# Expert 0's first 64 rows chosen on chip by matmul, and the token rows' scaling moved from VectorE to ScalarE, in an encoder layer with a mixture of experts

## The reference, cut to what matters

```
x = x + concat(attention outputs) @ w_out
h = rmsnorm(x) * ffn_norm
gl = h @ router_group + bias          # 4 groups, the best one
el = h @ router_expert + bias         # 32 experts, the best two of the 8 in that group
out = sum over the two of gate * (silu(h @ w_gate[e]) * (h @ w_up[e])) @ w_down[e]
y = rmsnorm(x + out) * final_norm
```

## Time and profile before

| | us |
|---|---|
| Runs (3): median, lowest, highest | 811.28, 810.48, 814.19 |
| The profiled execution: its own time | 814.31 |
| its span | 812.6 |
| TensorE busy in it | 721.4 |

### The profile page before, as it was taken

The page is one execution under the profiler, slowest core; times in us unless marked ns, Lnnn a source line. Parts: engine busy times, 40 slices in busy tenths (PEclk is TensorE's granted clock), DMA queues, the critical chain, the costliest instruction groups (busy, mean ns, idle before and its releaser), DMA issues. The chain is left out here.

```text
span 812.6 us, 12300 instructions
## 1 busy us (share of the span) xinstructions
PE 721.4 (89%) x3978; PEld 406.1 (50%) x3979; DVE 321.7 (40%) x900; ACT 214.0 (26%) x575; POOL 201.1 (25%) x478
## 2 busy tenths in 40 slices
PE   6799999999978999999999964999998999999910
PEld 3455544444455666665555543555554555555500
DVE  3853221100088988881555561111121112112138
ACT  2432210111176777771211110111110111111122
POOL 1133332220024230232001223441231434442110
PEclk9999999999999999999999976999998999999965
DMA  8702002000050000000892168899999989999856
GB/s 301 293 1 104 0 1 89 15 0 1 9 204 1 1 1 1 2 2 0 327 419 83 79 225 296 292 343 372 394 341 383 378 293 360 405 370 396 352 219 258
DMA packets 40824, 154.64 MB, mean 190 GB/s; under 512 B 9642, under 2 KB 10794, under 8 KB 31936
## 3 DMA queue, kind: packets, MB, share of 16 engines
q1 hardware_dynamic: 33120, 138.20, 45.3%
q0 software_dynamic: 7648, 15.75, 5.7%
HBM read 142.29 MB, written 20.03 MB: 200 GB/s over the span
## 5 line engine op out<-in xcount | busy, mean ns | idle before, releaser
L1405 PE MATMUL banks<-arena 128*128 128x512 f32 (+1 forms) x384 | 164.5, 582 | 10.2 <-DMA arena<-w_in 7.7
L1670 PE MATMUL banks<-arena 128*64 128x256 f32 x1280 | 155.2, 388 | 5.7 <-issue 2.4
L1670 PEld LDWEIGHTS banks<-arena 128*64 128x64 f32 x1280 | 96.1, 139 | 52.5 <-issue 13.8
L1405 PEld LDWEIGHTS banks<-arena 128*128 128x128 f32 x384 | 72.5, 194 | 86.4 <-issue 79.0
L1679 PE MATMUL banks<-arena 128*64 128x512 f32 x320 | 94.4, 609 | 0.5 <-ACT arena L980 0.5
L1561 PE MATMUL banks<-arena 128*128 128x512 f32 x192 | 86.4, 598 | 1.1 <-DVE arena L1162 1.1
L1326 DVE TENSOR_TENSOR arena<-arena,banks 128x128 f32<-128x128 f32 x40 | 11.5, 288 | 165.4 <-ACT arena L972 165.4
L1118 DVE TENSOR_REDUCE arena<-banks 128x1 f32<-128x512 f32 (+1 forms) x96 | 55.3, 598 | 48.5 <-PE banks L1477 41.5
L903 ACT ACTIVATE arena<-banks,arena 128x512 f32<-128x512 f32 (+1 forms) x96 | 58.2, 611 | 42.6 <-DVE arena L1121 20.6
L1561 PEld LDWEIGHTS banks<-arena 128*128 128x128 f32 x192 | 35.1, 190 | 38.8 <-issue 37.5
L972 ACT ACTIVATE arena<-banks 128x128 f32<-128x128 f32 x40 | 11.1, 277 | 159.0 <-PE banks L1670 159.0
(11 more groups left out here) (179 smaller groups left out, 855.6 us busy)
## 6 DMA issues: line engine op xcount, KB each, us to landing
arena<-w_gate SPq DMA_DIRECT2D x32, 1024.0 KB, 12.7
arena<-w_up SPq DMA_DIRECT2D x32, 1024.0 KB, 12.8
arena<-w_down SPq DMA_DIRECT2D x32, 1024.0 KB, 13.0
arena<-w_in SPq DMA_DIRECT2D x3, 2048.0 KB, 8.3
arena<-pair_rows SPq DMA_DIRECT2D x5, 1024.0 KB, 11.2
arena<-w_out SPq DMA_DIRECT2D x1, 4096.0 KB, 12.8
arena<-xT SPq DMA_DIRECT2D x6, 512.0 KB, 10.2
arena<-x SPq DMA_DIRECT2D x6, 512.0 KB, 10.5
```

The lines of the kernel that those rows point to most:

```text
L1405: last = nc.tensor.matmul(bank(mm % 2)[:, 0:GROUP_COLS[g]], xgT[:, t, c, :], w[:, c, :], start=(c == 0), stop=(c == DC - 1))
L1670: last = nc.tensor.matmul(bank(b)[h * SLOTS:(h + 1) * SLOTS, 0:2 * P].rearrange("p (g n) -> p g n", g=2), x_eT[i][:, c, :], w[:, :, c, h * ...
```

## The change

The store of scaled rows loses its gain and moves to ScalarE; the gain is multiplied in when rows are copied out behind their transposes. Expert 0's first 64 rows no longer come by a gather. For each tile, VectorE makes `select` (128 tokens x 64 slots): the one-hot slot, times the token's mask of expert 0, times its rs. TensorE multiplies x_tok by it, summed over six tiles in bank 4, the left 512 columns in partitions 0 to 63 and the right in 64 to 127. ScalarE copies that to x_sel; 16 matmuls with the identity transpose it; VectorE multiplies by the gain. On SP, expert 31's load is now issued ahead of the wait for the scattered lists and of their load. TensorE reads the counts behind the transposes of expert 1. The rest is the same; some tiles change places in SBUF (left out).

```diff
@@ SP
+                    sp.dma_start(gain_rows, A["ffn_norm"].rearrange("o (p c) -> (o p) c", c=DC)).then_inc(lam_loaded, 16)
...
-            sp.dma_start(gain_ffn, A["ffn_norm"].to_broadcast([P, D])).then_inc(gffn_in, 16)
...
             store_residual(NT - 1)
+            sp.wait_ge(x2_stored, NT * 16)
+            sp.wait_ge(h2_ready, NT)
+            sp.wait_ge(rms2_ready, NT)
+            sp.wait_ge(x2T_psum, 2 * NT)
+            sp.wait_ge(chosen_psum, 1)
+            load_expert(NGRP - 1, members(NGRP - 1)[-1])
             sp.wait_ge(ids_scattered, 2 * NT * 16)
             for h in range(2):
                 sp.dma_start(yids_sb[h * SLOTS:(h + 1) * SLOTS, NE:].rearrange("r (b e) -> r b e", e=NE),
                              ids_dram.rearrange("(b r e) o -> r b (e o)", b=NBLK, e=NE)[:, 1:, :]).then_inc(ids_loaded, 16)
-            sp.wait_ge(x2_stored, NT * 16)
-            sp.wait_ge(h2_ready, NT)
-            sp.wait_ge(rms2_ready, NT)
-            sp.wait_ge(x2T_psum, 2 * NT)
-            load_expert(NGRP - 1, members(NGRP - 1)[-1])
@@ GpSimd
-            gather_main(0, 0)
+            pool.sem_inc(id_ready, 1)
             gather_main(0, 1)
@@ ScalarE
+            def ffn_norm(t):
+
+                act.wait_ge(norm_ready, t + 1)
+                if t >= 2:
+                    act.wait_ge(h2_stored[t % 2], 16 * (t // 2))
+                act.activation(h2[t % 2].rearrange("n (c p) -> n c p", c=DC), x_tok[:, t, :].rearrange("n (p c) -> n c p", c=DC),
+                               ACT.Copy, scale=rs[:, t:t + 1]).then_inc(h2_ready, 1)
+
...
                 if t < NT - 1:
                     x2T_evac(t)
+                ffn_norm(t)
+            act.wait_ge(chosen_psum, 1)
+            act.activation(x_sel, bank(4), ACT.Copy).then_inc(chosen_rows, 1)
             act.wait_ge(gates_in, 1)
@@ VectorE
-                dve.wait_ge(lam_loaded, 6 * 16)
+                dve.wait_ge(lam_loaded, 7 * 16)
...
-            def ffn_norm(t):
+            def norm(t):
                 dve.wait_ge(rms2_ready, t + 1)
-                link(dve.reciprocal(rs[:, t:t + 1], rs[:, t:t + 1]))
...
-                dve.scalar_tensor_tensor(h2[t % 2].rearrange("n (c p) -> n c p", c=DC),
-                                         x_tok[:, t, :].rearrange("n (p c) -> n c p", c=DC), rs[:, t:t + 1],
-                                         gain_ffn.rearrange("n (p c) -> n c p", c=DC), ALU.mult, ALU.mult).then_inc(h2_ready, 1)
+                dve.reciprocal(rs[:, t:t + 1], rs[:, t:t + 1]).then_inc(norm_ready, 1)
+                dve.wait_ge(norm_ready, t + 1)
...
+            def choose(t):
+
+                for i, mask in enumerate((m1_all, m2_all)):
+                    dve.tensor_scalar(share[:, i:i + 1], mask[:, t, 0:1], rs[:, t:t + 1], None, ALU.mult).then_inc(dve_chain, 1)
+                    chain[0] += 1
+                dve.wait_ge(dve_chain, chain[0])
+                dve.wait_ge(onehot_ready, 2 * t + 2)
+                link(dve.tensor_scalar(select[:, t, :], onehot[:, 0, 0:SLOTS], share[:, 0:1], None, ALU.mult))
+                dve.scalar_tensor_tensor(select[:, t, :], onehot[:, 1, 0:SLOTS], share[:, 1:2], select[:, t, :],
+                                         ALU.mult, ALU.add).then_inc(select_ready, 1)
+
...
                 place(t)
+                choose(t)
...
             slots(NT - 1)
+            dve.wait_ge(xeT_psum, 1)
+            dve.tensor_tensor(x_eT[0], bank(0).rearrange("p (c n) -> p c n", c=DC), gain_eT, ALU.mult).then_inc(xeT_ready, 1)
 
             dve.wait_ge(counts_psum, 1)
...
-                        dve.tensor_copy(x_eT[(s + 1) % 2], bank(0).rearrange("p (c n) -> p c n", c=DC)).then_inc(xeT_ready, 1)
+                        dve.tensor_tensor(x_eT[(s + 1) % 2], bank(0).rearrange("p (c n) -> p c n", c=DC), gain_eT, ALU.mult).then_inc(xeT_ready, 1)
@@ TensorE
+            def choose(t):
+
+                pe.wait_ge(select_ready, t + 1)
+                for h in range(2):
+                    last = nc.tensor.matmul(bank(4)[h * SLOTS:(h + 1) * SLOTS, :], select[:, t, :],
+                                            x_tok[:, t, h * 512:(h + 1) * 512], start=(t == 0), stop=(t == NT - 1))
+                return last
...
             router(NT - 1, 1)
+            for t in range(3):
+                choose(t)
             rank(NT - 1)
-            counts = bank(1)[:, 0:NE]
+            choose(3)
+            place(NT - 1)
+            choose(4)
+            choose(5).then_inc(chosen_psum, 1)
+            counts = bank(2)[:, 0:NE]
...
-            place(NT - 1)
...
+                    if first and s == 0:
+                        pe.wait_ge(counts_ready, 1)
+                        words = load_counts(pe, g)
...
-            pe.wait_ge(rows_in[0], 16)
-            rows_transpose(0, 0, range(DC)).then_inc(xeT_psum, 1)
-            pe.wait_ge(counts_ready, 1)
+            pe.wait_ge(chosen_rows, 1)
+            x_sel_c = x_sel.rearrange("n (p c) -> n c p", c=DC)
+            for c in range(DC):
+                for h in range(2):
+                    half = slice(h * SLOTS, (h + 1) * SLOTS)
+                    last = nc.tensor.matmul(bank(0)[half, c * SLOTS:(c + 1) * SLOTS], x_sel_c[half, c, :], ident[half, half],
+                                            start=True, stop=True)
+            last.then_inc(xeT_psum, 1)
```

More of the change, by code:

```diff
@@ L180, in build @@
         K0 = R0 + DC * T
-        M0 = K0 + 1412
+        M0 = K0 + 1420
         x_tok = arena[:, X0:X0 + NT * D].rearrange("p (t d) -> p t d", t=NT)
@@ L222, in build @@
         gain_in = k.take(DC)
+        gain_rows = k.take(DC)
         gains = k.take(4)
@@ L269, in build @@
         m = Area(M0, WORDS)
+        x2T = m.take(D).rearrange("p (c n) -> p c n", c=DC)
         h2 = [m.take(D) for _ in range(2)]
-        x2T = m.take(D).rearrange("p (c n) -> p c n", c=DC)
-        gain_ffn = m.take(D)
+        onehot = m.take(2 * P).rearrange("p (i n) -> p i n", i=2)
+        select = m.take(NT * SLOTS).rearrange("p (t n) -> p t n", t=NT)
+        x_sel = m.take(512)
+        junk_c = m.take(256).bitcast(bf16)
+        slot_of = m.take(4 * NE).rearrange("p (i w e) -> p i w e", i=2, w=2)
+        ones = m.take(P)
         m1_all = m.take(NT * NE).rearrange("p (t e) -> p t e", t=NT)
@@ L275, in build @@
         macc = m.take(NT * NE).rearrange("p (t e) -> p t e", t=NT)
[L276 to L283, removed]
         r_g = m.take(3 * NG)
@@ L286, in build @@
         slot_f = m.take(2)
-        junk_c = m.take(256).bitcast(bf16)
+        rank_f = m.take(2)
+        bias_r = m.take(NG + NE)
+        top = m.take(1)
+        max_g, max_1, max_2 = (m.take(NT) for _ in range(3))
+        share = m.take(2)
         cnt = m.take(NE)
@@ L291, in build @@
         pk = m.take(NGRP * RING)
+        logit = m.take(NT * (NG + NE)).rearrange("p (t e) -> p t e", t=NT)
         m = Area(WORDS - DC * (NG + NE) - DC, WORDS)
@@ L328, in build @@
         router_in = sem("router_in")
-        gffn_in = sem("gffn_in")
+        norm_ready = sem("norm_ready")
         dve_chain = sem("dve_chain")
@@ L388, in build @@
         id_psum = sem("id_psum")
+        select_ready = sem("select_ready")
+        chosen_psum = sem("chosen_psum")
+        chosen_rows = sem("chosen_rows")
         slots_ready = sem("slots_ready")
@@ L1163, in _ @@
             dve.tensor_tensor(w_r, w_r, gain_cols.unsqueeze(2).to_broadcast([P, DC, NG + NE]), ALU.mult).then_inc(ones_ready, 1)
+            gain_eT = gain_rows.unsqueeze(2).to_broadcast([P, DC, SLOTS])
             def residual(t, h):
@@ L1261, in _ @@
                 x2T_evac(t)
-                ffn_norm(t)
+                norm(t)
                 route(t)
@@ L1276, in _ @@
             slots(NT - 1)
+            dve.wait_ge(xeT_psum, 1)
+            dve.tensor_tensor(x_eT[0], bank(0).rearrange("p (c n) -> p c n", c=DC), gain_eT, ALU.mult).then_inc(xeT_ready, 1)
             dve.wait_ge(counts_psum, 1)
-            link(dve.tensor_copy(cnt[0:1, :], bank(1)[0:1, 0:NE]))
+            link(dve.tensor_copy(cnt[0:1, :], bank(2)[0:1, 0:NE]))
             link(dve.memset(extra[0:1, :], 0.0))
@@ L1335, in further_rows @@
                 dve.wait_ge(e_xeT_psum, c + 2)
-                dve.tensor_copy(x_eT[2], bank(6).rearrange("p (c n) -> p c n", c=DC)).then_inc(e_xeT, 1)
+                dve.tensor_tensor(x_eT[2], bank(6).rearrange("p (c n) -> p c n", c=DC), gain_eT, ALU.mult).then_inc(e_xeT, 1)
             def dve_group(g):
@@ L1355, in dve_group @@
                             hT_evac(k + j + 1)
-            dve.wait_ge(xeT_psum, 1)
-            dve.tensor_copy(x_eT[0], bank(0).rearrange("p (c n) -> p c n", c=DC)).then_inc(xeT_ready, 1)
             gate_inputs()
@@ L1689, in transpose_rows @@
             def transpose_rows(g, s):
-                await_count(rows_in[s % RING], 16 * (g + s // RING + 1))
+                await_count(rows_in[s % RING], 16 * (g + s // RING + (s % RING >= 1)))
```

(11 more changed lines are left out.)

4 lines of the change are left out of this document (removed).

## The result

The changed kernel takes 818.38 us (median of 7 runs, 817.22 to 821.38); the kernel before, in 7 runs, 813.19 (810.48 to 817.48). The ratio is 1.0062, with a 95% interval of 1.0039 to 1.0084: 5 us slower. The forecast was +5.1 us, 816.4 on the scale of the three runs shown at first. The kernel before has since shown 813.19, and 813.19 + 5.1 = 818.3. The profiled execution took 818.38.

What follows compares the result with a forecast made beforehand. TensorE was taken as the bound, its hole between the stages winnable but ending in the wait for the lists: 0.1 early load + 2.9 lists + 2.1 clock = +5.1 us, 816.4 us; eight in ten from 810.5 to 820.

Steps and rivals of the forecast that it cites:

- What bounds the kernel: TensorE's hole between router and experts, 477.5 to 497.98, can be won; what stands ahead of expert 1's gate_up decides.
- Choosing: On TensorE between the stages: choosing ends between 485 and 489, gate_up of expert 0 starts 6.5 us earlier.
- The residual store: Tile 5's store on SP's queue lands late because it waits behind experts 4 and 5; expected at 495.2.
- The lists: On SP's queue behind expert 31's 3 MB load, they land at 507.2 instead of 502.1.
- What waits for them: ids_further on VectorE holds expert 1's copy and TensorE; gate_up of expert 1 starts at 508.7, +2.9 us.
- The clock: TensorE idles until 508.7, so gate_up of expert 1 runs at half clock, 5.79 in place of 3.67, +2.1 us.
- Later on: In the experts' stage from expert 6's load on, nothing absorbs the delay and nothing adds to it.
- The copies with the gain: The 39 other row copies become products with PSUM as source, 685 ns against 0.68: zero cost.
- The scaling: On ScalarE, 0.7 to 2.07 us a tile, taken as 1.2, hidden because TensorE is full for tiles 0 to 4.
- A: Rival on SP's queue: lists pass expert 31's load, land by 503.2; +1.0 us, 812.3; chance 0.17.
- B: Rival at expert 1: it waits for its own rows alone, gate_up at about 498, -7.8, 803.5; chance 0.10.
- C: Rival: choosing, strided transposes and clock make expert 0 late, mattering only if later than 501; chance 0.03.

Runs made afterwards that it cites:

- e1: Changed kernel with the two lists issued ahead of expert 31's load on SP's queue again: 812.61 us, ratio 0.9985 to the kernel before.
- e11: Changed kernel with the lists read later on VectorE and tile 5's residual store issued ahead of the loads of experts 4 and 5: 815.01 us, ratio 1.0012.
- e3: Changed kernel with the wait for the scatter and the two lists moved from SP's to ScalarE's queue: 819.99 us, ratio 1.0075.
- e9: Changed kernel with 14 filler products on unused data on TensorE while it waits for the lists: 818.97 us, ratio 1.0075.
- e7: Kernel before with only the scaling on ScalarE and the gain in the rows' copies, nothing chosen on chip: 813.41 us, ratio 0.9994.
- e8: The changed kernel itself, run again as a base: 818.21 us, ratio 1.0051 to the kernel before.
- e2: Kernel before with only expert 31's load moved ahead of the two lists on SP's queue: 819.67 us, ratio 1.0091.
- e6: Changed kernel with the lists issued ahead of expert 31's load and ids_further moved behind the copies on VectorE: 809.97 us, ratio 0.9954.
- e5: Changed kernel with VectorE's ids_further, which waits for the lists, moved behind the hidden copy of expert 1: 814.52 us, ratio 1.0019.

## Why the prediction was right, point by point

**What bounds the kernel.** Right: the hole between the stages was the place to win, and its second end decided. The 8.9 us won at expert 0 (behind t0) are worth 1.5 at R while the lists are read ahead of expert 1's rows (e1), and nothing where they are late.

**Choosing.** Forecast: over between 485 and 489, transposes 2.2 to 4.4 us, gate_up of expert 0 earlier by 6.5. Measured: over at 484.2, transposes 2.14, 10.0 earlier (8.9 from the end of the last router matmul, 20.4 against 11.6). My sum let the clock fall during choosing. With the wait for the mask filled, TensorE was idle for only 0.5 us in all there, and the clock stayed at 1.00 through it, in this execution and in the nine others that choose on chip. A tile took 0.93 to 1.08 us instead of 1.2 to 2.4. The clock fell only in 487:488 (0.69), behind the transposes, so that gate_up of expert 0 took 5.04. The misjudged term costs nothing, since the lists were the later end.

**The residual store.** Right in kind: it took 18.3 us behind 6 MB, and 2.9 us with nothing ahead (e11). Forecast to land 21.0 behind t0, it landed at 22.7 (19.5 after its issue at 476.32).

**The lists.** Right in size: forecast to be read 33.0 behind t0 (507.2), measured 34.3 (507.38): the store was 1.7 later, the loads and lists behind it 0.4 quicker. (My parts for expert 31 and the gathers add up to 506.5 and not to the 506 that I wrote; the forecast came from the 12.2 us of the other order.) The mechanism is right only in part. "The lists wait their turn in SP's ring" can't be the whole of it, since e3 took them out of that queue and they came no sooner.

A rule of the Trainium skill was at stake here ("DMA: Bandwidth & Descriptors", "Queues, rings and completion order"): that one row of rings is consumed in order, against the warning that completions are not in order. In the changed kernel the two lists came last, as the first would have it. The same section says that a DMA engine takes turns between the rows, packet by packet. That would not have saved the lists on a row of their own if the 1440 packets of the profile are what it counts by, against some 720 of expert 31, and e3's lists did land last; that these are the same packets no run here shows.

**What waits for them.** Right to the hundredth: 1.52 us from ids_further to gate_up of expert 1, as in the earlier trace rows. Forecast +2.9 at gate_up of expert 1; measured +4.2 from t0, the 1.3 above again.

**The clock.** Right in kind: 0.81 in 497:498, 0.50 until 513, 0.66 in 514:515. The one slow gate_up lasted 6.51 in place of 3.67, +2.8 where the forecast had +2.1.

**Later on.** The forecast was that the delay goes through unchanged. It does as far as R: 7.0 us behind at gate_up of expert 2 (4.2 + 2.8), 7.1 at G, 7.0 at R. TensorE's round of one expert is 6.38 us in both kernels (512.22 to 518.60 before, 518.11 to 524.49 after), and it never waits longer than 0.9 us in between. "Nothing absorbs the delay" was wrong at R, where 1.7 us come back: 5.3 at S, 5.1 at the end. Every kernel waits 2.4 to 3.0 us there for gathered rows, and what the clock does afterwards differs. Stretches of 10 us (PE alone), of the kernel before and of the changed one:

```profile
610.00:620.00 10.00, 7.32 (x31) 0.75 1.01 361
620.00:630.00 10.00, 10.00 (x66) 0.91 1.02 405
```

```profile
610.00:620.00 10.00, 8.87 (x56) 1.00 1.02 337
620.00:630.00 10.00, 7.60 (x49) 1.00 1.01 394
```

Before, the clock fell at the end of that wait and came back some 7 us later. In the changed kernel it held, and a second wait for gathered rows, of 1.38 us, followed at 630.21. From R to S it is 59.6 us before and 57.9 after. Among the others it is 59.5 and 59.6 in e9 and e7, which had long stretches at half clock there as well (0.70 and 0.68 over 10 us), and 57.9 to 58.7 in nine. In seven of these nine the clock fell for only some 3 to 4 us; in e3 and e8 it held, and a second wait of 1.51 and 1.74 us followed as in the changed kernel. So what costs here is the long stretch, and a clock that holds gains next to nothing over a short one. It points to the luck of an execution rather than to a property of the change: e9 is built as the changed kernel in this part and had the long stretch, e2 as the kernel before and had a short one. But the kernel before and e7, alike here, both had it, and with one execution each this isn't settled. The forecast's +5.1 met the measured +5.1 by cancellation: its terms for the lists and the clock were 1.3 and 0.7 too small, and in the pair profiled 1.9 us went the other way, 1.7 of them here. The ratio over all runs (+5 us) doesn't say how much of it holds on the average; that stays open.

**The rest.** The early load isn't seen: it lies ahead of t0, and 0.1 us is far less than t0 jitters. The copies with the gain take 0.69, as forecast. The scaling was forecast at 1.2 us out of 0.7 to 2.07 and takes 2.16, more than its range allowed; it is hidden by the cover named (e7).

**The rivals.** A (the lists pass the load): excluded, they took 9.5 us, and gate_up of expert 1 came at 508.90 where A had 504.7. B (faster, if the lists land before 496): did not come, but its mechanism is e6's, where expert 1 waits for its own rows alone and starts 7.2 us earlier behind t0 than in the kernel before (forecast 7.8). C (choosing makes expert 0 late): excluded, it started at 487.98, 13 us before the 501 from which it would matter.

## What to carry to other kernels

When a wait is taken away, look for what stands ahead of the *next* piece of work, and at whose expense it is ready: here two small lists, moved behind 3 MB, cost more than the wait that was removed had been worth. A small transfer that somebody waits for is issued before large ones, since another queue didn't protect it here, and it is read as late as the first use allows. The order alone won back the loss, the later reading alone about half of it, and both together made the change pay. And compare executions from an event ahead of the part of the change that is in question, when the stages before it jitter by as much as the effect.

## What the runs showed that was not expected

- Two lists in small pieces need 3.0 us on nearly free DMA engines (a share of 0.24 in 495:496 of e1), 9.4 to 9.6 behind a load of 3 MB in the same queue, 11.1 beside it in another queue, and 10.6 to 12.7 in e2, e5 and e11, where more was under way.
- ScalarE's scaling with a reordered read (128 x 1024 fp32, every eighth element) takes 2.16 us, where VectorE's product with the same read and a gain took 2.07, and a plain ScalarE pass over 1024 columns 1.06 (line 1040): half as long. That pass writes bf16, so the order of the read and the type written are not told apart. The Trainium skill ("SBUF — State Buffer", "Door 1: The DMA port swizzle") notes that accesses are fast while they stay in the same 16 bytes, four elements of fp32, and pay at each new line; the reordered read steps by 32 bytes. No run here isolates it.
- At one and the same wait of 2.4 to 3.0 us TensorE's clock fell in ten of thirteen executions and held in three (after, e8, e3). Where it stayed down for some 7 us (before, e7, e9) the stretch to S took 59.5 to 59.6 us, otherwise 57.9 to 58.7, whether it fell or held. A difference of a third of the effect studied can thus come from the execution alone.
- Matmuls on unused data keep the clock up for 12 us, with no gain in time that two such kernels in three sets of runs could show, and beside them the lists came about 1.0 us later each time.
